# Requesting the experts' down weights from ScalarE's DMA queue instead of SyncE's

## The reference

```python
def expert_block(xs):
    tok, g, e = xs
    xb = x_pad[tok]
    hb = jax.nn.silu(xb @ w_exp_gate[e]) * (xb @ w_exp_up[e])
    return (hb @ w_exp_down[e]) * g[:, None]
```

## Time and profile before

| | |
|---|---|
| median of 3 runs | 2172.23 us (2171.41 to 2173.5) |
| the profiled execution | 2176.87 us |
| its span, first to last instruction | 2175.1 us |
| PE busy | 1940.5 us (89%) |
| DVE busy | 1203.3 us (55%) |
| ACT busy | 952.8 us (44%) |
| POOL busy | 589.4 us (27%) |
| mean traffic | 201 GB/s |

### The profile page before, as it was taken

The page is one execution under the profiler, slowest core; times in us unless marked ns, Lnnn a source line. Parts: engine busy times, 40 slices in busy tenths (PEclk is TensorE's granted clock), DMA queues, the critical chain, the costliest instruction groups (busy, mean ns, idle before and its releaser), DMA issues. The chain is left out here.

```text
span 2175.1 us, 27110 instructions
## 1 busy us (share of the span) xinstructions
PE 1940.5 (89%) x8280; PEld 1332.8 (61%) x8280; DVE 1203.3 (55%) x2222; ACT 952.8 (44%) x1620; POOL 589.4 (27%) x435
## 2 busy tenths in 40 slices
PE   7989989976999997689998988979999999999992
PEld 3533435765777665367876876647766666666661
DVE  1755413526777774246164344447777777777663
ACT  2411214523666553356264222146655555555551
POOL 4799995101222222000000000012222222222221
PEclk9799989986999999789999999789999999999996
DMA  5353422351999994211202335229999999999983
GB/s 176 114 184 117 163 77 72 135 195 54 336 334 325 327 324 135 89 49 40 78 6 78 108 115 218 83 94 344 338 338 327 324 331 337 322 337 326 317 280 98
DMA packets 120530, 437.44 MB, mean 201 GB/s; under 512 B 31920, under 2 KB 36416, under 8 KB 83328
## 3 DMA queue, kind: packets, MB, share of 16 engines
q1 hardware_dynamic: 92760, 402.69, 50.2%
q0 software_dynamic: 27648, 33.67, 7.0%
q10 hardware_dynamic: 40, 0.05, 0.0%
HBM read 442.51 MB, written 63.48 MB: 233 GB/s over the span
## 5 line engine op out<-in xcount | busy, mean ns | idle before, releaser
L1528 DVE TENSOR_TENSOR big_parts<-big,h_cols_parts 128x1024 fp32r<-128x1024 f32 x384 | 460.1, 1222 | 126.9 <-ACT h_cols_parts L1581 118.4
L1581 ACT ACTIVATE h_cols_parts<-big 128x1024 fp32r<-128x1024 f32 x384 | 395.7, 1057 | 99.9 <-PE bank L1489 64.8
L1518 PE MATMUL bank<-big,heads 128*128 128x512 f32 x768 | 352.7, 602 | 1.5 <-ACT heads L1589 1.5
L1792 POOL DMA_INDIRECT acc_scratch<-heads,small x96 | 159.5, 1662 | 618.0 <-DVE small L1559 386.3
L1487 PE MATMUL bank<-h_cols_parts,heads_parts 128*128 128x512 f32 x768 | 312.7, 407 | 15.9 <-DVE heads_parts L1549 15.7
L1489 PE MATMUL bank<-h_cols_parts,heads_parts 128*128 128x512 f32 x768 | 304.0, 396 | 0.0
L1488 PE MATMUL bank<-big_parts,heads_parts 128*128 128x512 f32 x768 | 302.7, 394 | 0.0
L1518 PEld LDWEIGHTS bank<-big,heads 128*128 128x128 f32 x768 | 138.3, 190 | 139.8 <-issue 137.8
L1614 ACT ACTIVATE heads<-bank 128x512 f32<-128x512 f32 x96 | 57.4, 598 | 335.4 <-DMA acc_scratch<-heads,small 262.9
L1619 POOL MEMSET heads<- 128x2048 f32 x2 | 3.6, 1805 | 687.2 <-POOLq L1354 687.2
L1487 PEld LDWEIGHTS bank<-h_cols_parts,heads_parts 128*128 128x128 f32 x768 | 147.3, 192 | 47.7 <-DVE heads_parts L1549 11.3
(11 more groups left out here) (361 smaller groups left out, 3014.4 us busy)
## 6 DMA issues: line engine op xcount, KB each, us to landing
big<-in_w_exp_down_dram SPq DMA_DIRECT2D x96, 1024.0 KB, 14.2
big<-in_w_exp_gate_dram SPq DMA_DIRECT2D x96, 1024.0 KB, 7.1
big<-in_w_exp_up_dram SPq DMA_DIRECT2D x96, 1024.0 KB, 14.7
big<-in_w_in_dram SPq DMA_DIRECT2D x13, 2048.0 KB, 8.9
junk<-in_w_mod_dram SPq DMA_DIRECT2D x12, 1024.0 KB, 5.1
spare<-in_w_mod_dram SPq DMA_DIRECT2D x12, 1024.0 KB, 5.1
big<-in_w_out_dram SPq DMA_DIRECT2D x4, 2048.0 KB, 10.4
h_scratch<-h_rows SPq DMA_DIRECT2D x8, 512.0 KB, 7.6
```

Of the source, the lines that this page charges most:

```text
L1518: mm = pe.matmul(b_y[half][:, :], hidt[:, b, P * j:P * j + P], dn[q][:, j, 512 * half:512 * half + 512], start=j == 0, stop=j == FH - 1)
L1528: dve.tensor_tensor(gu_low[q][:, :, part, :], gu[q][:, :, part, :], gu_high[:, :, part, :].bitcast(F32), ALU.subtract).then_inc(w_low, 1)
L1581: act.activation(gu_high[:, :, part, :], gu[q][:, :, part, :], ACT.Copy).then_inc(w_high, 1)
L1792: return pool.indirect_dma_start(out=K.acc_dram, out_offset=bass.IndirectOffsetOnAxis(at, 0), in_=rows, in_offset=None, bounds_check=S - 1 ...
```

## The change

The function `down` takes the queue that is to issue its DMA. SP's program requests gate and up only. ACT's program requests down of expert i+2 in step i, right behind its copy of the right half of the down product of expert i-1 (L1614); the down product of expert i-1 is what frees the buffer. No semaphore is added: the waits that stand ahead of that copy cover the buffer.

```diff
-    def down(self, sp, e, q):
-        sp.dma_start(self.dn[q], self.w_down[expert1(e)]...).then_inc(self.d_in[q], 16)
+    def down(self, queue, e, q):
+        queue.dma_start(self.dn[q], self.w_down[expert1(e)]...).then_inc(self.d_in[q], 16)
...
         act.activation(ys[:, b, 512:1024], b_y[1][:, :], ACT.Copy).then_inc(y_act, 1)
+        if has(2):
+            weights.down(act, i + 2, (r + 2) % 3)
...
-            def both(e, r):
+            def gate_up(e, r):
                 sp.wait_ge(au_mm, e - 2)
                 weights.gate_up(sp, e, r % 3)
-                if late(e, 4):
-                    sp.wait_ge(y_mm, e - 3)
-                    weights.down(sp, e - 1, (r - 1) % 3)
...
-            sp.wait_ge(y_mm, E - 3)
-            weights.down(sp, E - 1, (E - 1) % 3)
```

More of the change, by code:

```diff
@@ L1245, in gate_up @@
             sp.dma_start(self.gu[q][:, g, :, :], w[at].rearrange("e (p c) f -> (e p) c f", p=P)).then_inc(self.gu_in[q], 16)
-    def down(self, sp, e, q):
-        sp.dma_start(self.dn[q], self.w_down[expert1(e)].rearrange("e (p j) d -> (e p) j d", p=P)).then_inc(self.d_in[q], 16)
+    def down(self, queue, e, q):
+        queue.dma_start(self.dn[q], self.w_down[expert1(e)].rearrange("e (p j) d -> (e p) j d", p=P)).then_inc(self.d_in[q], 16)
 def expert1(e):
@@ L1646, in _ @@
         def _(sp):
-            def both(e, r):
+            def gate_up(e, r):
                 sp.wait_ge(au_mm, e - 2)
                 weights.gate_up(sp, e, r % 3)
-                if late(e, 4):
-                    sp.wait_ge(y_mm, e - 3)
-                    weights.down(sp, e - 1, (r - 1) % 3)
             loops = (E - 4) // 3
-            both(3, 3)
+            gate_up(3, 3)
             with sp.Fori(0, loops, 1) as n:
                 for k in range(3):
-                    both(n * 3 + (4 + k), 4 + k)
+                    gate_up(n * 3 + (4 + k), 4 + k)
             for e in range(4 + 3 * loops, E):
-                both(e, e)
-            sp.wait_ge(y_mm, E - 3)
-            weights.down(sp, E - 1, (E - 1) % 3)
+                gate_up(e, e)
 def overflow_stage(K, tag, m, w_gate, w_up, w_down):
```

## The result

The changed kernel takes 2202.24 us (median of 4 runs, 2194.28 to 2208.87) against 2172.27 us: 1.36% slower, ratio 1.0136 with a 95% interval of 1.0108 to 1.0163. The forecast was 2204 us. The profiled execution took 2208.87 us around a span of 2207.2, 32.0 us more than the one before; it is the slowest of the four, so its figures show the effect a little large.

The account below looks back on a forecast made before the run. The prediction took the gapless scatter chain, its latency made by the weights' traffic, to pace the expert stages. It added 80 x 0.4 = +32 us to 2172 us, giving 2204 us, with 2157 to 2252 us for 8 in 10.

Parts of the forecast that it names:

- The pace is the scatter chain: Both expert stages: two scatters are never in flight, so a step takes scatter latency 10.2 us plus 0.85 us.
- somewhere never empty: Weights' line on the DMA engines: up lands 16.6 us after its request, longer than a step, so weights always queue somewhere.
- the faster rival: Down tied to a scatter's landing no longer flows beside the old scatter's last rows; latency falls, 2156 us; chance 0.18.
- SP's and ACT's issuing: SP loses 90 waits and requests, ACT gains 90 requests covered by its copy and waits: 0; uncovered, 36 us.
- The later request: Down goes out just after a scatter's landing instead of 1.2 to 2.0 us before; costs down itself nothing.
- The second line: Down on ACT's queue makes two weight lines beside the scatter's; 0.4 us more scatter latency a step, between 0 and 2.8.
- the thinning of the traffic: DMA engines: a longer step thins the weights' traffic, so the backlog drains over 11 us; used to take 0.4 from 1.4.
- A spare of about 10 us becomes 8: Down needs 15.7 us to land and is used 26 us later; the later request shortens that spare.
- No change: Queues share the DMA engines, bytes stay the same and the scatter doesn't notice the second line: 2172 us; chance 0.20.
- The full turn: Each row on the scatter's last engine waits for two weight rows: 1.4 us in 60 of 80 steps, 2256 us; chance 0.13.
- ACT late: ACT's request isn't covered where the scatter lands late, delaying silu and the last split: 36 us, 2208 us; chance 0.07.
- The rule of turns: Each DMA engine serves its queues a packet at a time in turn; the scatter's share falls from a half to a third.

Follow-up runs that it names:

- e4_no_down: Kernel before without the down weights of all experts but the first three of each stage: 2132.3 us in a single run.
- e6_half_rows: Kernel before with each weight request (gate, up and down) cut in two, so rows of 4 KB instead of 8 KB: 2191.0 us, ratio 1.0079.
- e12_act_down_half: Changed kernel with each down request cut in two by columns, so down in 4 KB rows on ACT's queue: 2193.8 us, 1.0079 of the kernel before.
- e5_act_burst: Against the kernel before, down requested on ACT's queue behind silu, when SP requests the next expert's gate and up: 2193.5 us, ratio 1.0095.
- e7_quarter_rows: Kernel before with each weight request cut in four, so rows of 2 KB: 2216.7 us, ratio 1.0190.

## Why the prediction was right, and where it was not

- **The pace is the scatter chain.** Right for before and after: 0.85 us from landing to issue in both, the period following the latency, and with the latency away (e4_no_down) PE's 10.2 us. But it isn't the only chain near its limit; the weights' own landing is the other one (e6_half_rows), which I had seen only as a line "somewhere never empty". I had weighed the faster rival by the chain's latency alone; that a shorter latency can come with a slower kernel wasn't in it.
- **SP's and ACT's issuing, priced at 0.** Right. 3.3 us of waits in 560 us on ACT, and with 36.9 us of them e12_act_down_half is faster than the change.
- **The later request, priced at 0.** Wrong, and this is the step that failed. I looked only at what down needs, and it had 10 us to spare. What the request's rows do to the scatter behind them is another question: on SP's queue alone this move, a little further (-0.2 us instead of -0.7), costs 1.16%. Moved some 7 us instead, it costs nothing.
- **The second line, priced at 0.4 us a step.** Its sign held, and the longer latency with it: 0.94% and 0.95% at two times on ACT's queue against 0.00% and -0.01% on SP's. That rows take turns is the reading that fits; no run shows a turn. By the periods it is 10.94 - 10.79 = 0.15 and 11.08 - 10.86 = 0.22 us, by the time 20 us / 80 = 0.25 us, about half of the 0.4. The whole change came to 11.32 - 10.79 = 0.53 us in the second stage and 0.30 in the first, so the sum fitted because a term that was too large stood for two. That 2204 met 2202 to 2 us is luck; the 0.4 was a choice between 0 and 1.4.
- **The two terms don't add** (20 and 23 us alone, 30 together by the medians). That fits the thinning of the traffic that I had used to choose 0.4 from 1.4: at a period of 11.32 us the DMA share is down to 91% from 94%. No run tests it.
- **"A spare of about 10 us becomes 8"**: it became larger, as down lands in 7.7 us. It doesn't wait behind gate and up any more.
- **The rivals.** No change and faster are out: the latency rose by 0.5 us. The full turn wanted 1.4 us more in most steps. ACT late is out by the 3.3 us and by e12_act_down_half.
- **The rule of turns.** The Trainium skill ("DMA: Bandwidth & Descriptors", "Queues, rings and completion order") has each DMA engine go round between its queues. e12_act_down_half (half the row, 12 us less) and e6_half_rows (half the row, 0.9 us less latency) agree with it. The rule on the same page that issuing from several engines only saves sequencer time ("Issuing engines are not separate DMA queues") would have given no change; here the queue alone cost 20 us (e5_act_burst), as a third party, the scatter, shares the engines with both queues.

## What to carry to other kernels

With the DMA engines 94% busy, as here, the choice of queue decides who waits: the weights moved to a second queue and those that stood behind them arrive sooner, and the small transfers of a third queue arrive later. So look first for a chain of short transfers that wait for each other. A request with time to spare isn't free to move; ask which transfer it will run beside. And when a latency falls while the kernel gets slower, look for the second chain that now waits.

## What the runs showed of the hardware that I had not expected

- Latency under load bends sharply: the same scatters land in 6.1 us after the last weights, in 6.2 us with two thirds of the weights and the DMA engines 71% busy (e4_no_down), and in 10.2 us with all of them and 94%.
- A landing is that of the slowest of 16 parts. In the kernel before (1540 to 2090 us) 15 of the 16 parts of a down request have landed after 10.3 us and the last after 15.7 (medians, from the steps of its semaphore in the trace); for up it is 13.0 and 16.7, and for a scatter the parts land anywhere between 3.3 and 10.2 us. So the line that is "never empty" seems to be that of a few engines.
- The down request on SP's queue costs 23 us when it goes out 0.2 us ahead of the scatter's issue, and nothing 2 to 3 us ahead or right behind gate and up. Why just that place is dear isn't settled; no run separates down's rows from the scatter's first ones. In that run and in the change the request is also released by a scatter's landing, in the two that cost nothing by a product of PE; place and releaser were never changed apart.
- Halving a request by partitions (64 each) raised the DMA engines' time per 8 KB row from 0.38 to 0.61 us, and the kernel is 12% slower than before; halving it by columns took 12 us off the change.
- Rows of 4 KB cost the engines little more by themselves: 78.0% for 165.00 MB before is 42 us of engine time per MB, and 78.9% for 162.51 MB (e6_half_rows) is 43 or 44; rows of 2 KB, 81.2% for 156.17 MB (e7_quarter_rows), take 47.
- The rows of the second queue aren't dearer as such: in the change 27.3% for 52.43 MB is 47 us per MB, but in e5_act_burst 23.6% for 53.49 MB is 40, less than on SP's queue.
